# Splitting fp32 weights into two halves: the low half by GpSimd's subtraction or by an accumulating DMA

## The reference, cut to what matters

```python
h = x * (1.0 + scale[:, None]) + shift[:, None]
proj = h @ w_in[l]                      # (512, 2048) @ (2048, 6144)
...                                     # A gated convolution, B attention, C RG-LRU, D S5 + GLU
y = jnp.concatenate([y_a, y_b, y_c, y_d], axis=-1) @ w_out[l]    # (512, 2048) @ (2048, 2048)
x = layer_norm(ALPHA * x + (1.0 + gate) * y)
```

## Time and profile before

| | |
|---|---|
| median of 3 runs | 2152.26 us (2152.07 to 2152.48) |
| the profiled execution, its span | 2154.4 us |
| TensorE matmul busy | 1850.3 us (86%) |
| TensorE weight loads busy | 1366.0 us (63%) |
| VectorE busy | 1515.3 us (70%) |
| ScalarE busy | 546.3 us (25%) |
| GpSimd busy | 683.6 us (32%) |
| DMA queue of SP, share of 16 engines | 40.3%, 272.36 MB |

### The profile page before, as it was taken

One profiled execution on the slowest core, in us unless ns is written; L12 is line 12 of the kernel. 1 busy time (PEld: TensorE's weight loads), 2 busy tenths in 40 slices (PEclk: granted clock), 3 DMA queues, 4 the chain that ended last, 5 costly groups with the idle time before them and its releaser, 6 DMA issues.

```text
span 2154.4 us, 24427 instructions
## 1 busy us (share of the span) xinstructions
PE 1850.3 (86%) x7335; PEld 1366.0 (63%) x7335; DVE 1515.3 (70%) x2383; ACT 546.3 (25%) x796; POOL 683.6 (32%) x341
## 2 busy tenths in 40 slices
PE   2229898899899989969997989998999998979994
PEld 1117566667666766656885756775776775757883
DVE  5787897799789869972324588578668839852755
ACT  2103222322222223222112322322332222232111
POOL 2115232323332232322443523332332333223441
PEclk9558898999899989979998889999998999989997
DMA  7786225524642552353333423421342342234432
GB/s 269 246 288 181 78 80 178 162 82 132 184 126 79 175 161 87 112 161 128 97 98 127 121 74 103 123 90 59 103 130 67 99 121 83 71 100 149 164 98 88
DMA packets 294715, 273.25 MB, mean 127 GB/s; under 512 B 23928, under 2 KB 220896, under 8 KB 291560
## 3 DMA queue, kind: packets, MB, share of 16 engines
q1 hardware_dynamic: 294632, 272.36, 40.3%
HBM read 261.81 MB, written 10.51 MB: 126 GB/s over the span
## 4 chain that ended last, share of the span: by engine, by line
PE 43%; DVE 41%; issue 6%; DMA 6%; SPq 3%; POOL 1%; DVEq 1%; ACT 0%; POOLq 0%
DVE work L1126 13%; PE bank L728 12%; PE bank L729 12%; PE bank L730 12%; DVE ada_acc L1134 7%; DMA ada_in<-in_w_ada 4%; DVE work L1006 3%; DVE work L1005 2%; DVE work L1134 2%; DVE work L1130 2%; DVE y_t L1134 2%; PE bank L869 1%; DVE carry L1134 1%; PE bank L756 1%; DVE carry L1126 1%
## 5 line engine op out<-in xcount | busy, mean ns | idle before, releaser
L484 POOL TENSOR_TENSOR w_lo<-raw,w_hi 128x1024 fp32r<-128x1024 f32 x256 | 629.8, 2461 | 1274.0 <-ACT w_hi L536 1274.0
L728 PE MATMUL bank<-op_hi,w_hi 128*128 128x512 f32 x1536 | 639.8, 417 | 5.1 <-POOL w_lo L484 5.1
L729 PE MATMUL bank<-op_lo,w_hi 128*128 128x512 f32 x1536 | 618.9, 403 | 0.0
L730 PE MATMUL bank<-op_hi,w_lo 128*128 128x512 f32 x1536 | 616.7, 401 | 0.0
L536 ACT ACTIVATE w_hi<-raw 128x1024 fp32r<-128x1024 f32 x256 | 270.8, 1058 | 1178.7 <-PE bank L730 1129.4
L728 PEld LDWEIGHTS bank<-op_hi,w_hi 128*128 128x128 f32 x1536 | 302.6, 197 | 122.6 <-issue 53.2
L730 PEld LDWEIGHTS bank<-op_hi,w_lo 128*128 128x128 f32 x1536 | 300.5, 196 | 67.6
L729 PEld LDWEIGHTS bank<-op_lo,w_hi 128*128 128x128 f32 x1536 | 301.9, 197 | 61.5 <-issue 1.9
L1134 DVE SCALAR_TENSOR_TENSOR ada_acc<-ada_in,cond,ada_acc 128x512 f32<-128x512 f32 (+1 forms) x256 | 258.1, 1008 | 50.8 <-DMA ada_in<-in_w_ada 33.4
L728 PE MATMUL bank<-w_hi,op_hi 128*128 128x512 f32 x512 | 200.0, 391 | 0.0
L729 PE MATMUL bank<-w_lo,op_hi 128*128 128x512 f32 x512 | 199.2, 389 | 0.0
(11 more groups left out here) (188 smaller groups left out, 1747.3 us busy)
## 6 DMA issues: line engine op xcount, KB each, us to landing
raw<-in_w_in SPq DMA_DIRECT2D x192, 512.0 KB, 4.0
ada_in<-in_w_ada SPq DMA_DIRECT2D x256, 256.0 KB, 3.8
raw<-in_w_out SPq DMA_DIRECT2D x64, 512.0 KB, 3.7
raw<-in_w_ada SPq DMA_DIRECT2D x24, 512.0 KB, 5.1
ada_in<-in_w_ada SPq DMA_DIRECT2D x16, 512.0 KB, 5.7
bias_t<-in_w_ada SPq DMA_DIRECT2D x8, 512.0 KB, 5.1
work<-in_w_ada SPq DMA_DIRECT2D x8, 512.0 KB, 6.0
rot<-in_w_ada SPq DMA_DIRECT2D x8, 512.0 KB, 6.1
```

The lines of the kernel that those rows point to most:

```text
L484: pool.tensor_tensor(w_lo[:, n % NHL, :], raw[:, n % NRAW, :], w_hi[:, n % NHL, :].bitcast(F32), ALU.subtract).then_inc(s.lo_done.sem, 1)
L728: pe.matmul(out_, xh, wh, start=first, stop=False)
L729: pe.matmul(out_, xh, wl, start=False, stop=False)
L730: return pe.matmul(out_, xl, wh, start=False, stop=last)
```

## The change

The low half is no longer made by GpSimd's arithmetic. ACT, after its rounded copy `w_hi = raw`, makes a second copy `w_lo = -raw`, rounded alike, so minus the high half. GpSimd then issues a DMA from `raw` to `w_lo` that adds to what lies there, which gives raw - high. TensorE waits for `hi_done` alone, runs the 16 passes of a half that read `w_hi`, gives `w_hi` back (`hi_used`), waits for the DMA's landing (`lo_in`), and runs the 8 passes that read `w_lo`. The raw slot is given back (`raw_used`) by the first of those 8, no longer by the split. GpSimd's loop over the steps is written out.

```diff
-            s.lo_done = signal("lo_done" + n, HALF, NRAW)
+            s.hi_used = signal("hi_used" + n, HALF, NHL)
+            s.neg_done = signal("neg_done" + n, HALF)
+            s.lo_in = [signal(f"lo_in{i}" + n, HALF // NHL * 16) for i in range(NHL)]
+            s.raw_used = signal("raw_used" + n, HALF, NRAW)
...
                         if n != HALF - 2:
-                            sp.wait_ge(s.lo_done.sem, ct * HALF + (n + 1 + (n == HALF - 3)))
+                            sp.wait_ge(s.raw_used.sem, ct * HALF + (n + 1 + (n == HALF - 3)))
...
-                    pool.wait_ge(s.hi_done.sem, s.hi_done.at(n + 1, step) + ahead * HALF)
-
-                    pool.wait_ge(s.mm_done.sem, s.mm_done.at(n + 1 - NHL, step) + ahead * HALF)
-                    pool.tensor_tensor(w_lo[:, n % NHL, :], raw[:, n % NRAW, :],
-                                       w_hi[:, n % NHL, :].bitcast(F32), ALU.subtract).then_inc(s.lo_done.sem, 1)
+                    pool.wait_ge(s.neg_done.sem, s.neg_done.at(n + 1, step) + ahead * HALF)
+                    pool.dma_start(w_lo[:, n % NHL, :], raw[:, n % NRAW, :], accum_op=ALU.add)\
+                        .then_inc(s.lo_in[n % NHL].sem, 16)
...
                     act.wait_ge(slot.sem, slot.at(16 * (n // NRAW + 1), step) + ahead * slot.per)
+                    act.wait_ge(s.hi_used.sem, s.hi_used.at(n + 1 - NHL, step) + ahead * HALF)
+                    act.activation(w_hi[:, n % NHL, :], raw[:, n % NRAW, :], ACT.Copy).then_inc(s.hi_done.sem, 1)
+
                     act.wait_ge(s.mm_done.sem, s.mm_done.at(n + 1 - NHL, step) + ahead * HALF)
-                    act.activation(w_hi[:, n % NHL, :], raw[:, n % NRAW, :], ACT.Copy).then_inc(s.hi_done.sem, 1)
+                    act.activation(w_lo[:, n % NHL, :], raw[:, n % NRAW, :], ACT.Copy, scale=-1.0)\
+                        .then_inc(s.neg_done.sem, 1)
...
-                        pe.wait_ge(s.lo_done.sem, s.lo_done.at(n + 1, ct))
+                        pe.wait_ge(s.hi_done.sem, s.hi_done.at(n + 1, ct))
+                        o = bank[u % 2][:, :]
                         for j in range(KH):
-                            k = half * KH + j
+                            k, w = half * KH + j, slice(P * j, P * (j + 1))
                             if u == 0:
                                 pe.wait_ge(s.op_lo.sem, k + 1)
-                            w = slice(P * j, P * (j + 1))
-                            mm = product(bank[u % 2][:, :], (w_hi[:, n % NHL, w], w_lo[:, n % NHL, w]),
-                                         (op_hi[:, k, :], op_lo[:, k, :]), k == 0, k == KT - 1)
+                            pe.matmul(o, w_hi[:, n % NHL, w], op_hi[:, k, :], start=k == 0, stop=False)
+                            mm = pe.matmul(o, w_hi[:, n % NHL, w], op_lo[:, k, :], start=False, stop=False)
+                        mm.then_inc(s.hi_used.sem, 1)
+
+                        lo_ready(n, ct)
+                        for j in range(KH):
+                            k, w = half * KH + j, slice(P * j, P * (j + 1))
+                            mm = pe.matmul(o, w_lo[:, n % NHL, w], op_hi[:, k, :], start=False, stop=k == KT - 1)
+                            if j == 0:
+                                mm.then_inc(s.raw_used.sem, 1)
                         mm.then_inc(s.mm_done.sem, 1)
```

More of the change, by code:

```diff
@@ L342, in _ @@
                 else:
-                    sp.wait_ge(layers[l - 1].lo_done.sem, layers[l - 1].lo_done.at(W_OUT, CT))
+                    sp.wait_ge(layers[l - 1].raw_used.sem, layers[l - 1].raw_used.at(W_OUT, CT))
                 with sp.Fori(0, CT) as ct:
@@ L387, in _ @@
                     chunk, kk = n // 8, n % 8
-                    sp.wait_ge(s.lo_done.sem, s.lo_done.at(n + 1 - NRAW, CT))
+                    sp.wait_ge(s.raw_used.sem, s.raw_used.at(n + 1 - NRAW, CT))
                     sp.dma_start(raw[:, n % NRAW, :].rearrange("p (k n) -> p k n", k=2),
@@ L477, in _ @@
             for l, s in enumerate(layers):
-                pool.sem_inc(s.lo_done.sem, NRAW)
+                pool.sem_inc(s.raw_used.sem, NRAW)
                 def split_lo(n, step, ahead=0):
-                    pool.wait_ge(s.hi_done.sem, s.hi_done.at(n + 1, step) + ahead * HALF)
-                    pool.wait_ge(s.mm_done.sem, s.mm_done.at(n + 1 - NHL, step) + ahead * HALF)
-                    pool.tensor_tensor(w_lo[:, n % NHL, :], raw[:, n % NRAW, :],
-                                       w_hi[:, n % NHL, :].bitcast(F32), ALU.subtract).then_inc(s.lo_done.sem, 1)
+                    pool.wait_ge(s.neg_done.sem, s.neg_done.at(n + 1, step) + ahead * HALF)
+                    pool.dma_start(w_lo[:, n % NHL, :], raw[:, n % NRAW, :], accum_op=ALU.add)\
+                        .then_inc(s.lo_in[n % NHL].sem, 16)
                 for k in range(KT):
@@ L493, in _ @@
                                        ALU.subtract).then_inc(s.op_lo.sem, 1)
-                with pool.Fori(0, CT) as ct:
+                for step in range(CT):
                     for n in range(2, HALF):
-                        split_lo(n, ct)
-                    split_lo(0, ct, 1)
-                    split_lo(1, ct, 1)
+                        split_lo(n, step)
+                    split_lo(0, step, 1)
+                    split_lo(1, step, 1)
                 for n in range(2, W_OUT):
@@ L720, in _ @@
                 pe.sem_inc(s.mm_done.sem, NHL)
+                pe.sem_inc(s.hi_used.sem, NHL)
                 if l:
@@ L723, in _, with lo_ready @@
                     channels(s, range(KT))
[L725 to L730, removed]
+                def lo_ready(n, step):
+                    slot = s.lo_in[n % NHL]
+                    pe.wait_ge(slot.sem, slot.at(16 * (n // NHL + 1), step))
                 with pe.Fori(0, CT) as ct:
@@ L884, in _ @@
                         pe.wait_ge(s.gb.sem, 4)
-                    pe.wait_ge(s.lo_done.sem, s.lo_done.at(n + 1, CT))
+                    pe.wait_ge(s.hi_done.sem, s.hi_done.at(n + 1, CT))
                     for t in range(ST):
@@ L892, in _ @@
                                 pe.wait_ge(s.op_lo.sem, KT + k + 1)
-                            x_, w_ = slice(P * t, P * (t + 1)), slice(S * j, S * (j + 1))
-                            mm = product(bank[4 * (c % 2) + t][:, :], (op_hi[:, k, x_], op_lo[:, k, x_]),
-                                         (w_hi[:, n % NHL, w_], w_lo[:, n % NHL, w_]), k == 0, k == KT - 1)
+                            o, x_, w_ = bank[4 * (c % 2) + t][:, :], slice(P * t, P * (t + 1)), slice(S * j, S * (j + 1))
+                            pe.matmul(o, op_hi[:, k, x_], w_hi[:, n % NHL, w_], start=k == 0, stop=False)
+                            mm = pe.matmul(o, op_lo[:, k, x_], w_hi[:, n % NHL, w_], start=False, stop=False)
+                    mm.then_inc(s.hi_used.sem, 1)
+                    lo_ready(n, CT)
+                    for t in range(ST):
+                        for j in range(2):
+                            k = 2 * kk + j
+                            o, x_, w_ = bank[4 * (c % 2) + t][:, :], slice(P * t, P * (t + 1)), slice(S * j, S * (j + 1))
+                            mm = pe.matmul(o, op_hi[:, k, x_], w_lo[:, n % NHL, w_], start=False, stop=k == KT - 1)
+                            if t == 0 and j == 0:
+                                mm.then_inc(s.raw_used.sem, 1)
                         if kk == 7 and t < ST - 1:
```

## The result

The changed kernel takes 2191.7 us (median of 4 runs, 2190.27 to 2194.06), the kernel before 2152.16 beside it. The ratio is 1.0189, 95% interval 1.0176 to 1.0202: 1.9% slower, outside the forecast range and on the other side. The profiled execution has a span of 2188.6 us, 34.2 above that of before.

The account below looks back on a forecast made before the run. TensorE and VectorE were taken to hold each other up in turn, above TensorE's floor of about 162 us a step. 2154.4 - 4 x 13 - 4 x 17 + 5 - 4 + 10 = 2045, forecast 2043 us, range 1990 to 2170.

Parts of the forecast that it names:

- Bounds and floor: Steps: TensorE and VectorE hold each other up; TensorE's floor about 162 us a step, layer 0 32 above, layer 1 19.
- (1): 256 GpSimd subtractions go: VectorE gets 250 to 300 us back, some 30 a step, leading only to TensorE's floor.
- (2): 256 negated copies come on ACT, 271 us, taking it from 25% to some 38%; costed at 0.
- (3): Adding DMA into w_lo: lands within its budget, no stall in the mean; 10 us in all for collisions with w_ada loads.
- X: Time from the end of ACT's negation to the adding DMA's landing as TensorE sees it: 6.5 us, up to 8.0 allowed.
- Rival B: Adding DMA is slow: at X = 12, 2.0 us more on each output-projection half; time 2285, chance 0.20.
- (4): Raw slots free 5.7 us later, SP's queue slips: 3 us stall at step start (5 layer 0), 3 at layer-0 ends.
- Rival C: VectorE's sums wait for later w_ada loads, layer 0 gaining 5 us a step instead of 17; time 2090, chance 0.15.
- (5): TensorE's new order: last chunk's row tiles come late, +2.7 us a layer, +5 in all.
- Rival D: GpSimd's DMA issuing holds the shared port about as long as the subtraction, VectorE not freed; time 2165, chance 0.08.

Follow-up runs that it names:

- small_landing: Changed kernel with SP waiting for the adding DMA's landing to reuse raw slots, step loop written out, DMA cut to 128 of 1024 columns: 1986.27 us, 0.9230.
- order_early: Kernel before with TensorE running the 16 w_hi passes first; GpSimd still subtracts and gives the raw slot back: 2156.88 us, ratio 1.0023.
- order_late: As order_early, but the raw slot is given back by TensorE's first pass with w_lo: 2250.77 us, 1.0445 of the kernel before.
- small_dma: Changed kernel with the adding DMA cut to 128 of 1024 columns, same waits and signals: 2133.09 us, 0.9905 of the kernel before.
- steps_only: Changed kernel, slots back at landing; output projections from their third tile use GpSimd's subtraction and TensorE's old order: 2076.09 us, 0.9637.
- the square: Changed kernel, slot back at TensorE's pass or at landing: 2191.7 and 2103.7 us with whole DMA, 2133.1 and 1986.3 with an eighth.
- plain_copy: Changed kernel with a plain copy from raw to w_lo in place of the adding DMA: 2154.93 us, 1.0007 of the kernel before.

## Why the prediction was wrong, point by point

**Bounds and floor: right.** TensorE's floor of 162 us a step was close: small_landing reaches 165 and 169 with no stall worth naming, and the table of windows shows it busy throughout. Its 1986 us is close to the 1990 that I gave as the end without stalls.

**(1) VectorE's relief: right in mechanism and size.** 250 to 300 us forecast, 300 measured; 0.692 and 0.752 us where 0.69 and 0.75 were named. What I left out is that the same late load costs more when its user is fast. The waits of the `ada_acc` sums in order_early and in small_landing:

```profile
DVE ada_acc L1145 <- DMA ada_in<-in_w_ada: 32.4, 36, 10.0
...
DVE ada_acc L1156 <- DMA ada_in<-in_w_ada: 75.5, 52, 10.0
```

With early slots they are 32 us with a slow VectorE and 76 with a fast one. With late slots they are 178 (order_late) and 191 to 228 (small_dma and the changed kernel). So most of the 228 us is lateness, which a slow VectorE meets too. In time the late slot costs 94 us beside a slow VectorE (order_early to order_late) and 147 beside a fast one (small_landing to small_dma); the two pairs differ in how the low half is made as well, so this is no clean measure of VectorE's part.

**(2) ACT's copies: right**, at nothing: small_landing has them all and comes near TensorE's floor.

**(3) The DMA: right in latency, wrong in what was asked of it.** X was forecast at 6.5 us with 8.0 to spare; the median landing was 4.9, and TensorE's direct waits for it are small (21.5 us in the steps, 12.1 in the output projections). Rival B's price, with X = 12 and 2.0 us on every half, is out; its sign, waits of TensorE on this DMA in the output projection, shows at a small size. But I weighed the transfer by its landing alone and never added its engine time to the shares of before. One transfer has 144 packets of 0.317 us in the mean, on 16 engines 2.9 us, so 0.52 of a half's 5.44. In the last output projection, where SP also loads the residual, the share was 0.63 before already, and the sum is over 1. First the kernel before, then the changed one, columns as in the earlier trace rows, and two of TensorE's waits in that stretch:

```profile
1985.00:2030.00 45.00, 45.00 (x200) 37.28 (x199) 26.88 (x28) 8.63 (x9) 21.69 (x9) 1.00 0.63 215
...
2000.00:2052.00 52.00, 42.50 (x178) 32.60 (x177) 14.20 (x21) 14.06 (x14) 6.62 (x8) 1.00 1.00 300
...
2003.41 2.11 PE L915 MATMUL bank<-w_lo,op_hi 128*128 128x512 f32 x8 [1.65 <-DMA w_lo<-raw]
2010.21 2.11 PE L915 MATMUL bank<-w_lo,op_hi 128*128 128x512 f32 x8 [1.07 <-DMA w_lo<-raw]
```

DMA share 1.00, and the half between these two takes 6.80 us, not 5.44, while SP loads the residual and the norm's rows (1 MB each). The two projections grew by 3.9 and 12.3 us, which the forecast had at 0 inside a general allowance of 10. steps_only gives them back. In the steps the traffic has a share too: taking seven eighths of it away gained 59 us from the changed kernel (small_dma), where giving the slots back at the landing gained 88.

**(4) The late slot: the step that failed.** I saw the slip, put it at 5.7 us for the slot, 3 at the step's start and 6 to 9 for the `w_ada` loads, and then priced it at 3 us of stall at L743 (5 in layer 0) and 3 at a layer-0 step's end. order_late measures it by itself: +94 us in all, 18.7 a step in layer 0. Three errors are in it. At the start the parameters slipped by 4.4 us, not 3, and took 1.7 longer to VectorE, so the stall grew to 6.7 us (9 to 10 in layer 0) instead of shrinking to 3 (5). In the middle I counted nothing, and there the circle of SP, VectorE and TensorE costs a stall of 9.4 to 9.7 us in each layer-0 step. And TensorE is at 1.2 GHz after such a stall: for 153 us of layer 0's input projection, against 122 before (in layer 1 it is 34 against 72). A layer-0 step took 206.9 us instead of 177, one of layer 1 took 174.3 instead of 168. In spans, the forecast was 109 us below the kernel before and the result 34 above it. Of these 143 us, 113 are layer 0's steps and what follows to its output projection (-68 forecast, +45 measured), 24 are layer 1's (-52 and -28), and 6 the projections (10 and 16). The medians lie 149 apart, since spans and medians differ by 2 to 3 us. How the 137 us of the steps divide between late slots and traffic depends on which is taken away first (the square).

**Rival C named this feed** and gave it -5 us a step at a chance of 0.15. Its argument against, that the ring's pace is VectorE's own, fails because the loads stand in SP's one queue behind raw loads which wait for TensorE. Its price started from the relief and took some away, and the range ended near no change. An end for a step without relief and with the slip was missing; order_late measures that at 2251 us.

**(5) The late row tiles: right for the last layer**, +2.7 us at the end (29.4 to 32.1). Layer 0 shows none: from its last output matmul to the first of layer 1 it is 34.1 us before and in order_early, 34.0 in the changed kernel. So the term of +5 was about twice too large.

**Rival D is out:** GpSimd's issue of 0.86 us blocks nothing that VectorE's groups show.

The Trainium skill (Collectives: The Full Stack, The bandwidth ceiling) says that an addition inside a DMA costs no cycles but a second read, and so half a copy's rate. plain_copy agrees: 0.162 against 0.317 us a packet. The Trainium skill also has the rule (SBUF — State Buffer, Summary: rules for kernel authors) that a two-input VectorE operation and a GpSimd operation that reads SBUF block each other. The runs agree, with 300 us of VectorE's time. The Trainium skill's advice in the same section, against hiding a GpSimd-issued DMA under VectorE, changed nothing that these runs show: the 256 issues took 0.859 us in the median and at most 1.08, and the median landing of 4.9 us is close to the shortest of 4.5.

## What to carry to other kernels

When an edit moves the point where a buffer is given back, list everything that stands behind the load of that buffer in its queue, and price the wait of each against the engine as it will be after the change, not as it is; the same late slot cost 94 us beside the slow VectorE and 147 beside the fast one. Give a buffer back at the event that really ends its use (here the DMA's landing, and not the consumer's next step): that was worth 88 us and turned 1.9% slower into 2.2% faster. A DMA that adds counts twice in the engines' share, so add the shares by stage before using it, and use it only in stages where the engine that it relieves is busy: both together made the kernel 3.6% faster than before.

## What the runs showed of the hardware

A DMA from SBUF to SBUF of 512 KB in rows of 4 KB, issued by GpSimd, landed 3.0 us after its issue as a copy and 4.9 us as an addition (medians). The issue took 0.53 us of GpSimd's time as a copy and 0.86 us as an addition (medians). For the addition this does not go by size: 0.86 us for 64 KB, which landed in 2.4 us, and 0.87 us for 256 KB, which landed in 3.3. Halving a GpSimd subtraction from 128x1024 to 128x512 took its time from 2.46 to 1.59 us only and left VectorE with about three quarters of the time that it lost by blocking.
